# A float32 two-layer trunk on one core: the expert dispatch and the end reordered

## The reference

```python
x = x + rms_norm(mix, norm_g[layer, 1])
hn = rms_norm(x, norm_g[layer, 2])
ffn = moe_swiglu(hn, ...)            # router logits, top 2 of 8, softmax gates,
                                     # out += gates[:, e] * swiglu(hn, w_gu[e], w_down[e])
x = x + rms_norm(ffn, norm_g[layer, 3])
gate = sigmoid(x @ ple_w_gate[layer])
x = x + gate * (p[layer] @ ple_w_proj[layer])
```

## Time and profile before

| | us |
|---|---|
| median of 3 runs | 1585.31 |
| lowest and highest | 1583.36, 1587.27 |
| the profiled execution | 1587.94 |
| span of that execution's trace | 1586.2 |
| PE busy in the span | 1514.4 |
| DVE busy | 1282.8 |
| ACT busy | 1013.6 |
| mean granted PE clock | 0.976 |

### The profile page before, as it was taken

The page is one execution under the profiler, slowest core; times in us unless marked ns, Lnnn a source line. Parts: engine busy times, 40 slices in busy tenths (PEclk is TensorE's granted clock), DMA queues, the critical chain, the costliest instruction groups (busy, mean ns, idle before and its releaser), DMA issues.

```text
span 1586.2 us, 24059 instructions
## 1 busy us (share of the span) xinstructions
PE 1514.4 (95%) x7070; PEld 1264.7 (80%) x7070; DVE 1282.8 (81%) x1590; ACT 1013.6 (64%) x1278; POOL 10.7 (1%) x26
## 2 busy tenths in 40 slices
PE   7999999999976699999999999999999999999996
PEld 6777888788866688888888888888888888878875
DVE  6986554675876699989988988999899998988974
ACT  6555443464224477777867877877777777777752
POOL 1000000000000000000000000000000000000000
PEclk9999999999977799999999999999999999999998
DMA  7666556362323599989989989989989989999940
GB/s 274 207 217 226 174 186 203 111 226 81 125 75 117 195 338 360 366 332 376 353 334 369 357 333 362 380 314 379 368 311 383 370 307 375 378 332 338 368 167 27
DMA packets 120947, 439.92 MB, mean 277 GB/s; under 512 B 13632, under 2 KB 13632, under 8 KB 120912
## 3 DMA queue, kind: packets, MB, share of 16 engines
q1 hardware_dynamic: 119664, 435.25, 74.9%
q0 software_dynamic: 1248, 4.23, 0.8%
HBM read 438.38 MB, written 1.05 MB: 277 GB/s over the span
## 4 chain that ended last, share of the span: by engine, by line
PE 90%; DVE 6%; ACT 2%; issue 1%; DMA 1%; SPq 0%; DVEq 0%; ACTq 0%
PE PS L393 28%; PE PS L395 27%; PE PS L394 27%; PE PS L623 2%; DVE w_lo L1139 2%; PE PS L746 1%; PE PS L706 1%; PE PS L720 1%; DMA raw<-in_w_in_ab 1%; DVE xT_lo L1595 1%; PE PS L721 1%; ACT xT_hi L1062 1%; DVE xT_lo L1209 0%; DVE nr L1165 0%; PE PS L443 0%
## 5 line engine op out<-in xcount | busy, mean ns | idle before, releaser
L1139 DVE TENSOR_TENSOR w_lo<-raw,w_hi 128x1024 fp32r<-128x1024 f32 x486 | 567.5, 1219 | 36.0 <-ACT w_hi L819 32.6
L393 PE MATMUL PS<-w_hi,xT_hi 128*128 128x512 f32 x1424 | 567.7, 399 | 8.6 <-DVE xT_lo L1207 4.2
L395 PE MATMUL PS<-w_lo,xT_hi 128*128 128x512 f32 x1424 | 557.7, 392 | 0.0
L394 PE MATMUL PS<-w_hi,xT_lo 128*128 128x512 f32 x1424 | 556.9, 391 | 0.0
L819 ACT ACTIVATE w_hi<-raw 128x1024 fp32r<-128x1024 f32 x486 | 490.4, 1061 | 76.3 <-PE PS L395 52.2
L1139 DVE TENSOR_TENSOR w_lo<-SC,w_hi 128x1024 fp32r<-128x1024 f32 x340 | 391.5, 1218 | 14.6 <-ACT w_hi L819 14.5
L819 ACT ACTIVATE w_hi<-SC 128x1024 fp32r<-128x1024 f32 x340 | 337.6, 1061 | 38.0 <-PE PS L395 33.4
L393 PEld LDWEIGHTS PS<-w_hi,xT_hi 128*128 128x128 f32 x1424 | 269.9, 190 | 64.7 <-issue 4.4
L395 PEld LDWEIGHTS PS<-w_lo,xT_hi 128*128 128x128 f32 x1424 | 268.8, 189 | 57.9
L394 PEld LDWEIGHTS PS<-w_hi,xT_lo 128*128 128x128 f32 x1424 | 269.6, 189 | 53.8
L393 PE MATMUL PS<-w_hi,hT_hi 128*128 128x512 f32 x536 | 208.8, 389 | 2.6 <-DVE hT_lo L1344 2.6
(11 more groups left out here) (224 smaller groups left out, 746.8 us busy)
## 6 DMA issues: line engine op xcount, KB each, us to landing
raw<-in_e_w_gu SPq DMA_DIRECT2D x226, 512.0 KB, 6.5
SC<-in_e_w_gu SPq DMA_DIRECT2D x222, 512.0 KB, 6.5
raw<-in_e_w_down SPq DMA_DIRECT2D x112, 512.0 KB, 6.0
SC<-in_e_w_down SPq DMA_DIRECT2D x112, 512.0 KB, 5.6
raw<-in_ffn_w_gu SPq DMA_DIRECT2D x44, 512.0 KB, 5.0
raw<-in_w_in_c SPq DMA_DIRECT2D x32, 512.0 KB, 5.4
raw<-in_ffn_w_down SPq DMA_DIRECT2D x22, 512.0 KB, 5.2
raw<-in_w_in_ab SPq DMA_DIRECT2D x20, 512.0 KB, 6.5
```

The costliest lines, as they stand in the source:

```text
L393: pe.matmul(out, a_hi, b_hi, start=start, stop=False, skip_group_check=True)
L394: pe.matmul(out, a_lo, b_hi, start=False, stop=False, skip_group_check=True)
L395: return pe.matmul(out, a_hi, b_lo, start=False, stop=stop, skip_group_check=True)
L1139: dve.tensor_tensor(w_lo[:, g % RING, part], raw_part(g, s), w_hi[:, g % RING, part].bitcast(F32), ALU.subtract).then_inc(lo_done, 1)
```

## The change

- **Tile 1's chain.** On DVE the low parts of granules 74 and 75 no longer stand ahead of tile 1's weighing; 74 goes behind `add_y(3, 1)`, 75 and 76 go behind the selection and the gathered rows, 77 behind the tables. On ACT `hi(74)` goes ahead of tile 0's `xT`, `scale_x(0)` ahead of tile 1's, and `square_x(1)` behind it.
- **Router.** `wr_hi` and `wr_lo` lie side by side, so that two matmuls do the work of three; PE waits for each half of `xT` by itself. DVE adds the two halves of the logits (two more instructions).
- **Tables.** The first comparison is made straight from `slot`; gates and extra-item tables go behind `xg(1)`. PE reads the number of items behind the first `unit_gu`. ACT runs one Silu on a single column ahead of `xg(1)`.
- **Newton steps.** `root` uses SCALAR_TENSOR_TENSOR with one scalar in place of TENSOR_SCALAR with two.
- **End.** The order on PE becomes `unit_turn`, last down product (its left half finished six matmuls before its right), scatter, projection, `turn_x(4, 0)`, gates, with `turn_x(4, 1)` two granules earlier than before. The copy to `ye`, the addition to `acc` and its squares go by halves of 512 columns. Projection weights become granule 42 of the item and are loaded behind the last two. Stores go by halves.

```diff
@@ SP
                 else:
-                    load_proj(1, G_MOE + ITEM - 2, i * EU)
-                    unit_down(G_MOE + ITEM - 1, e, EU - 1, i * EU)
+                    unit_down(G_MOE + ITEM - 2, e, EU - 1, i * EU)
+                    load_proj(1, G_MOE + ITEM, i * EU)
...
-                sp.wait_ge(x_ready, x_count(5, t, 1))
-                sp.dma_start(out_d[0, t * P:(t + 1) * P, :], x[:, t, :]).then_inc(stored, 16)
+                for c in range(2):
+                    sp.wait_ge(x_ready, x_count(5, t, c))
+                    sp.dma_start(out_d[0, t * P:(t + 1) * P, c * N:(c + 1) * N],
+                                 x[:, t, c * N:(c + 1) * N]).then_inc(stored, 16)
@@ PE
-                pe.wait_ge(xT_ready, 2 * (5 * T + t + 1))
                 for k in range(KT):
-                    m = split_matmul(PS[:, 0, t * E:(t + 1) * E], xT_hi[:, k, tok], xT_lo[:, k, tok],
-                                     wr_hi[:, k, :], wr_lo[:, k, :], k == 0, k == KT - 1)
+                    if k % HK == 0:
+                        pe.wait_ge(xT_ready, 2 * (5 * T + t) + k // HK + 1)
+                    o = 2 * E * t
+                    pe.matmul(PS[:, 0, o:o + 2 * E], xT_hi[:, k, tok], wr_split[:, k, :], ...)
+                    m = pe.matmul(PS[:, 0, o:o + E], xT_lo[:, k, tok], wr_hi[:, k, :], ...)
...
+            def last_down(g, n, turns):
+                pe.wait_ge(hT_ready, n)
+                for j, r, c in ((0, 0, 0), (0, 0, 1), (0, 1, 0), (0, 1, 1), (1, 0, 0), (1, 1, 0), (1, 0, 1), (1, 1, 1)):
...
                 if last:
                     pe.wait_ge(selT_ready, i + 2)
-                    pe.wait_ge(pT_ready, 2)
-                    for kk in range(2):
-                        proj_half(1, G_MOE + ITEM - 2, kk, i * EU)
-                    unit_down(G_MOE + ITEM - 1, i * EU + (FB + EU), True, i * EU)
+                    last_down(G_MOE + ITEM - 2, i * EU + (FB + EU), i * EU)
...
+            unit_gu(G_MOE, 0, 2)
             pe.wait_ge(table_ready, 1)
             last_item = pe.value_load(...)
-            unit_gu(G_MOE, 0, 2)
...
-            pe.wait_ge(ye_ready, last_item + 2)
-            scatter(1)
+            for t, c in ((0, 0), (0, 1), (1, 0), (1, 1)):
+                if t == 0:
+                    pe.wait_ge(ye_ready, last_item + (c + 2))
...
+            pe.wait_ge(pT_ready, 2)
+            for kk in range(2):
+                proj_half(1, G_MOE, kk, last_item * EU + EU)
             turn_x(4, 0, True)
-            ple_gate(G_MOE + 1, 4, 6 * T, [], True, last_item * EU + EU)
+            for t in range(T):
+                for j in range(4):
+                    if t == 0 and j == 2:
+                        turn_x(4, 1, True)
+                    seg(G_MOE + 1 + j, OUT_FINAL + j // 2, j % 2, t, ...)
@@ ACT, dispatch
             square_x(0)
+            hi(74)
             xT(0, 5, V_N12)
-            his(74, 76)
             for c in range(2):
                 product(G_OUTC + 2 + 2 * c)
                 square_psum(1, c)
-            act.wait_ge(x_ready, x_count(3, 1, 1))
+            scale_x(0)
+            xT_half(1, 5, V_N12, 0)
+            xT_half(1, 5, V_N12, 1)
             square_x(1)
-            xT(1, 5, V_N12)
-            for t in range(T):
-                scale_x(t)
-            his(76, 78)
+            hi(75)
+            scale_x(1)
             act.wait_ge(lg_max, 1)
             act.activation(..., ACT.Exp)
+            hi(76)
+            act.activation(sg[:, 0:1], ones[:, 0:1], ACT.Silu)
             xg(1)
-            act.wait_ge(table_ready, 1)
-            last_item = act.value_load(...)
+            hi(77)
@@ DVE, root
-                    step(dve.tensor_scalar(a, y, y, h, ALU.mult, ALU.mult))
-                    step(dve.tensor_scalar(y, a, 1.5, y, ALU.add, ALU.mult))
+                    step(dve.scalar_tensor_tensor(out=a, in0=y, scalar=y, in1=h, op0=ALU.mult, op1=ALU.mult))
+                    step(dve.scalar_tensor_tensor(out=y, in0=a, scalar=1.5, in1=y, op0=ALU.add, op1=ALU.mult))
@@ DVE, dispatch
             norm_x(3, 0)
-            los(74, 76)
             for c in range(2):
                 weigh_psum(1, c, 4)
             stats_y(2, 1)
             add_y(3, 1)
+            lo(74)
             xT(1, 5, V_N12)
             norm_x(3, 1)
-            los(76, 78)
             dve.wait_ge(lg_done, 1)
...
+            dve.wait_ge(cnt_done, 1)
+            step(...)                      # slot, two instructions
+            for t in range(T):             # compare with slot itself
+                m = dve.tensor_scalar(sel[:, t, :], iota_c[:, :], slot[:, t * E:t * E + 1], None, ALU.is_equal)
+            m.then_inc(sel_ready, 1)
+            step(...)                      # over
+            lo(75)
+            step(...)                      # slots into the table
+            select(1)
+            xg(1)
+            lo(76)
...                                        # gates, extra-item tables, value_load
+            lo(77)
@@ DVE, end
+            add_acc(0)
+            weigh_acc(0)
+            stats_y(3, 0)
+            add_y(4, 0)
+            add_acc(1)
+            xT(0, 6, None, True)
+            weigh_acc(1)
+            stats_y(3, 1)
+            add_y(4, 1)
+            lo(G_MOE + 4, last_item * EU + EU)
+            embed_half(1, 0, 0)
+            xT(1, 6, None, True)
+            embed_half(1, 0, 1)
+            embed(1, 1)
```

More of the change, by code:

```diff
@@ L1090, in item @@
                     unit(u, False)
+                unit(EU - 2, not last)
                 if last:
                     pT(2)
-                unit(EU - 2, not last)
-                for q in ((4,) if last else (4, 5, 6)):
-                    hi(G_MOE + ITEM + q, i * EU)
+                else:
+                    for q in (4, 5, 6):
+                        hi(G_MOE + ITEM + q, i * EU)
             hi(G_MOE + 6)
             product(G_MOE + 4)
+            act.wait_ge(table_ready, 1)
+            last_item = act.value_load(itab[0:1, 0:1], min_val=E - 1, max_val=ITEMS - 1)
             with act.Fori(0, last_item) as i:
@@ L1177, in weigh_y @@
                 dve.wait_ge(gain_full, 16 * gains)
[L1178 removed]
+                m = dve.tensor_tensor(yx[:, t, c, :] if gains == 5 else yg[t][:, c, :], src, gain[:, c * N:(c + 1) * N], ALU.mult)
                 emit(m)
@@ L1526, in _, with select, compare, xg @@
             gates = rt[:, 320:320 + T * E]
+            slot = rt[:, 96:96 + T * E]
+            emit(dve.memset(tab[:, 0, :, :], -1.0))
+            emit(dve.memset(tab[:, 1, :, :], 0.0))
+            dve.wait_ge(cnt_done, 1)
+            step(dve.scalar_tensor_tensor(out=slot, in0=PS[:, 1, 0:T * E], scalar=1.0, in1=chosen, op0=ALU.add, op1=ALU.mult))
+            step(dve.tensor_scalar(slot, slot, -1.0, None, ALU.add))
+            for t in range(T):
+                m = dve.tensor_scalar(sel[:, t, :], iota_c[:, :], slot[:, t * E:t * E + 1], None, ALU.is_equal)
+            m.then_inc(sel_ready, 1)
+            over, place, one, tmp = (rt[:, 336 + k * E:336 + (k + 1) * E] for k in range(4))
+            step(dve.tensor_scalar(over, PS[:, 1, T * E:(T + 1) * E], float(P), None, ALU.is_gt))
+            lo(75)
+            step(dve.tensor_copy(tab[:, 0, :, 1:E + 1], slot.rearrange(tE, t=T)))
+            def select(col):
+                dve.tensor_copy(cur[:, 0, :].unsqueeze(2), tab[:, 0, :, bass.ds(col, 1)]).then_inc(cur_step, 1)
+            def compare():
+                for t in range(T):
+                    m = dve.tensor_scalar(sel[:, t, :], iota_c[:, :], cur[:, 0, t:t + 1], None, ALU.is_equal)
+                m.then_inc(sel_ready, 1)
+            def xg(n):
+                for b in range(2):
+                    dve.wait_ge(xg_act, n * 2 + (b - 1))
+                    for j in range(HK):
+                        k = HK * b + j
+                        m = dve.scalar_tensor_tensor(out=xT_lo[:, k, 0:P], in0=PS[:, 6 + b, j * P:(j + 1) * P],
+                                                     scalar=vcol[:, V_N12 + k:V_N12 + k + 1],
+                                                     in1=xT_hi[:, k, 0:P].bitcast(F32), op0=ALU.mult, op1=ALU.subtract)
+                    m.then_inc(xg_ready, 1)
+            select(1)
+            xg(1)
+            lo(76)
             dve.wait_ge(lg_exp, 1)
@@ L1532, in _ @@
                                    ALU.mult))
[L1534 to L1556 removed]
+            step(dve.tensor_copy(tab[:, 1, :, 1:E + 1], gates.rearrange(tE, t=T)))
             head = rt[:, 368:368 + 2 + XTRA]
[L1558 removed]
             step(dve.tensor_tensor(pair, later, by_col(over), ALU.mult))
@@ L1638, in item @@
                     unit(u, False)
+                unit(EU - 2, not last)
                 if last:
                     pT(2)
-                unit(EU - 2, not last)
-                for q in ((4,) if last else (4, 5, 6)):
-                    lo(G_MOE + ITEM + q, i * EU)
-            xg(1)
+                else:
+                    for q in (4, 5, 6):
```

(1 more changed line is left out.)

139 lines of the change are left out of this document (77 added, 62 removed).

## The result

The changed kernel takes 1565.55 us (median of 4 runs, 1564.07 to 1568.11), the kernel before beside it 1584.34 us (4 runs, 1583.28 to 1587.27). The ratio is 0.988, with a 95% interval from 0.9861 to 0.990. That is 18.8 us faster; the forecast was 1565.2. The profiled execution took 1565.99 us with a span of 1564.2.

The account below looks back on a forecast made before the run. PE and the weight stream were taken as full in the expert stage, leaving dispatch and end to gain. Savings of 8.8, 10.7 and 0.6 sum to 20.1 us, taking 1585.3 to 1565.2, range 1560 to 1573.

Parts of the forecast that it names:

- Steps 1 to 3: Dispatch, tile 1's chain through router and logits to gather: add_y at 499.3, router 504.1, gather 514.3 in place of 525.29.
- step 1: Dispatch, tile 1's chain on DVE: -4.6 for lo halves, +0.8 for hi(74), -0.9 for three roots, -4.7 us in all.
- Step 4: Dispatch, gather to first product: with tables out of the way it starts at 520.45, 12.6 us earlier, and ends at 531.6.
- Step 5: Dispatch, tables behind xg on DVE: unit_turn at 538.3, PE idles 6.7 us, 3.8 given back, leaving -8.8 us.
- rival C: Dispatch: DVE's new stretch is longer, each lo more costing 2.3 us; with two more, 1570; chance 0.08 shared with B.
- Steps 6 to 8: End, down product first, then scatter and gates: gates at 1547.1, -8.6 us, and -2.1 if the clock holds; sum -10.7.
- The sum: Whole kernel: 8.8 for the dispatch, 10.7 for the end and 0.6 for the last store, 20.1 us.
- A, the clock: Rival: the clock falls in the new end; one fall +3.0 us, 1568.2, or +13, 1578, if half throughout; chance 0.17.
- B: Rival: the weight stream holds the dispatch back, so only the end gains, 1574; chance 0.08 shared with rival C.
- D: Rival: the stream, not PE, paces the experts; each of 56 units takes 0.45 more, 25 us, 1590; chance 0.03.

Follow-up runs that it names:

- tables ahead: Changed kernel with gates, tables and the load of the counts back ahead of the second half of the gathered rows; 1567.57 us, ratio 0.9893.
- dispatch alone: Kernel before with only the dispatch part of the change, root and end as before; 1577.72 us, ratio 0.995.
- filled kernel: Changed kernel with weight splits, gates and table work moved into DVE's idle stretches of the dispatch; 1560.17 us, ratio 0.9846.
- split 74 ahead: Changed kernel with the split of weight column 74 back ahead of tile 1's weighing and root; 1566.91 us, ratio 0.9885.
- filled kernel without the early Silu: Changed kernel with DVE's idle dispatch stretches filled and ACT's early one-column Silu left out; 1562.71 us, ratio 0.9856.
- root alone: Kernel before with only the root's new Newton instructions; 1584.03 us, ratio 0.9993.

## Why the prediction was right, by its steps

**Steps 1 to 3** held within 1 us: `add_y` at 498.62 (forecast 499.3), router at 503.39 (504.1), counts at 510.19 (510.8), gather at 513.58 (514.3). All are early by the same 0.6 to 0.7, and A itself, ahead of the change, was 0.65 earlier in this execution (489.08, 489.73 before). Counted from A they hold within 0.1 us. Inside step 1 two errors nearly cancel. `hi(74)` ahead of `xT` made the subtraction 0.4 us later and not 0.8 (491.27 - 489.08 against 491.54 - 489.73), and of the three roots counted at 0.3 only two, of 0.33 each, stand between A and `add_y`. PE's wait for x of tile 1 was 4.85 us, where about 4 was given as a sign. The count that opens the prediction, four idles of PE within 16 us, does not come out of the earlier trace rows, which have three within 18 and five within some 40; no term uses it.

**Step 4** said 520.45 for the first product; it was 519.72, and ended at 530.9 (531.6).

**Step 5** was the longest sum and the one that rival C doubted: 16.0 us of DVE between `xg` and `unit_turn`, an idle of PE of 6.7 us, -8.8 in all. Measured were an idle of 6.90 and an A to B that is 8.7 us shorter. The terms as listed add up to 16.0; the "22.3 - 6.3" written beside them is not their sum. The reason given was right, too: filling DVE's gaps moved `unit_turn` by 3.9 to 4.7 us, and leaving out ACT's early Silu moved nothing. The two restarts of the clock did not cost quite the same: it was at half for 6.0 us behind B before and for 4.5 in the changed kernel, and the first unit took 25.55 and 24.89 us. One thing was not in the step. It treats the tables' new place as the source of part of the gain, and the tables ahead cost only some 2 us by the trace. With the tables ahead A to B is 51.30, so 6.1 of the 8.7 us come from the rest: tile 1's chain, the router and the splits that no longer stand between it, the logits and the gather. How they share it was not measured, but for the root's 0.9 and split 74.

**Steps 6 to 8.** From `unit_turn` to the down product 2.14 us (forecast 2.04), to the gates 18.70 (18.0). The gates are 7.9 us nearer to the last `unit_turn`, where the sum had 8.6: the copy of x through ACT and DVE took 1536.76 - 1534.29 = 2.47 us from turn to matmul and not 2.05, and the turn itself stood 16.2 us behind `unit_turn` and not 15.8, half of it in the scatter and half ahead of it. The chain of x under the projection was 1.1 us shorter than its cover (forecast 0.8). The clock and the store gave 3.0 us (G to end), where the steps had 2.1 and 0.6. Together 10.9 and not 11.3. In the list of DMA issues, the stores of the changed kernel:

```profile
out<-x SPq DMA_DIRECT2D x4, 256.0 KB, 2.0
```

0.6 us less to landing than in the earlier trace rows, the value taken.

**The sum** was 20.1 us; the two stretches measured 8.7 + 10.9 = 19.6. The medians gave 18.8 and 18.1, within their uncertainty. That the median came within 0.4 us of the forecast is in part luck: run again it was 1567.10, and the kernel before stood 1 us lower beside it than in the forecast. The profiled pair gave 22.0. Of the 2.4 us beyond the two stretches, 0.65 stand ahead of A, 0.66 in the first unit of item 0, and 1.0 between that and C, where this execution of before had the long fall of the clock at the last item and that of after a short one.

**The rivals.** A, the clock: it didn't fall in the new end, with idles of 1.51, 0.62 and 1.43 us in it and a granted clock of 1.00 throughout. By the Trainium skill's page "TensorE: Matmul & The Clock Gate", section "A second HAM failure mode: psum-queue depth-cycling", frequent short idles are enough for a swing; in these rows they weren't. B: A to B fell by 8.15 with the dispatch alone and B to C did not grow, so the stream held nothing back. C: the idle in question was 6.90 us against 6.7, with no split more than counted. D: the units of an item follow each other at 16.84 us in all kernels, as before.

## What to carry to other kernels

When one engine's list sets a stall, moving work within the part that it works off without a pause gains little (the place of the tables was worth some 2 us). What gains is moving work into the waits that stand ahead of the stall, until another engine sets it: here DVE's waits held 5.7 us, and filling them gave 3.9 to 4.7. An edit has to be judged where it works. The distance between two events of the bottleneck engine repeated to 0.1 us at the end and to 0.2 in the dispatch here, save where the clock came back at another place (0.9), while whole runs differed by 4. And a preparation such as an early table load is worth only what the chain around it has no slack for, so it should be measured again when that chain changes.

## What was unexpected of the hardware

The length of an idle of PE did not settle what the clock did. Windows of 2 us (PE, PEld, DVE, ACT, POOL, clock, DMA share, GB/s) behind an idle of 2.38 us, first with the tables ahead, then in the filled kernel:

```profile
540.00:542.00 2.00, 1.68 (x14) 1.68 (x15) 1.74 (x3) 2.00 (x3) 0.00 (x0) 1.00 0.00 0
```

```profile
532.00:534.00 2.00, 1.84 (x10) 1.84 (x11) 1.74 (x3) 2.00 (x3) 0.00 (x0) 0.69 0.93 270
534.00:536.00 2.00, 2.00 (x12) 2.00 (x11) 2.00 (x3) 2.00 (x4) 0.00 (x0) 0.50 0.94 358
```

The idle has one length, and the work ahead of it is the same product, started at the half clock in the first kernel and at the full one in the second. The clock stayed in the first and fell in the second. At the last item an idle of 1.90 us led to a fall in the changed kernel also, over some three windows of 1 us in place of six in the earlier trace rows. With the tables ahead the same code behind the same idle kept the full clock. Windows of the changed kernel, then PE alone with the tables ahead, where the idle ends at 1413.99:

```profile
1412.00:1413.00 1.00, 0.64 (x2) 0.59 (x3) 0.97 (x3) 1.00 (x2) 0.00 (x0) 0.86 1.04 414
1413.00:1414.00 1.00, 1.00 (x4) 0.72 (x3) 0.00 (x0) 1.00 (x2) 0.00 (x0) 0.50 0.76 303
...
1416.00:1417.00 1.00, 0.00 (x0) 0.00 (x0) 1.00 (x1) 0.26 (x1) 0.00 (x0) 0.93 0.00 0
```

```profile
1414.00:1415.00 1.00, 1.00 (x4) 1.00 1.02 406
1415.00:1416.00 1.00, 1.00 (x5) 1.00 0.74 295
```

Where the clock falls and comes back varies from execution to execution, and the record ties most of the 4 us between runs to it. Ahead of A, with nearly the same code, the traces show PE 13.7 us at the half clock in four kernels (A at 487.6 to 488.2), 17.1 us in five (489.0 to 489.9) and 20.5 us in five (490.2 to 491.6). At the last item there is no fall with the tables ahead and with split 74 ahead (B to C 978.30 and 978.85), one of 3.4 us in ten kernels (979.4 to 980.3), and one of 6.8 us in before and in the filled kernel without the early Silu (981.98 and 981.74). And of the 17 executions of the kernel before that ran beside the first experiments, the four fastest (1583.25 to 1583.63 us) have a mean granted clock of 0.980 or 0.981 and the two slowest (1587.38 and 1588.05) one of 0.976. It does not account for everything: the 11 executions of the root alone differ by 4.3 us at mean clocks of 0.977 and 0.978. All this was found in the traces; no run forced a fall or prevented one. What decides at idles near 2 us stays open.
